# Latent attention with scores keys-on-partitions in split passes, query maxima as an operand row, row sums from ones beside the values

## The reference, cut to what matters

```python
def mla_queries(cq, g_q, w_uq, w_qr, rope):
    cq = rms_norm(cq, g_q)
    q_nope = (cq @ w_uq).reshape(b, n, MLA_HEADS, MLA_NOPE_DIM)      # 8 heads x 64
    q_rope = (cq @ w_qr).reshape(b, n, MLA_HEADS, MLA_ROPE_DIM)      # 8 heads x 32
    ...                                                              # rotated for latent tokens
def softmax_attend(q, k, v, scale):
    s = jnp.einsum('bqhd,bkhd->bhqk', q, k, preferred_element_type=jnp.float32) * scale
    p = jax.nn.softmax(s, axis=-1).astype(v.dtype)
    return jnp.einsum('bhqk,bkhd->bqhd', p, v)
```

## Time and profile before

| what | us |
|---|---|
| three runs, median (lowest, highest) | 3573.81 (3564.94, 3577.81) |
| the profiled execution, its own time | 3574.6 |
| its span, first to last instruction | 3572.5 |
| busy over the span: PE / PEld / DVE / ACT / POOL | 3058.5 / 2406.8 / 1741.1 / 1198.9 / 506.9 |
| granted TensorE clock, mean of the span | 0.918 of full |
| latent attention, first layer: setup, prologue, main part | 14.3, 9.6, 145.8 |
| latent attention, second layer | 15.7, 7.9, 124.0 |

### The profile page before, as it was taken

One profiled execution on the slowest core, in us unless ns is written; L12 is line 12 of the kernel. 1 busy time (PEld: TensorE's weight loads), 2 busy tenths in 40 slices (PEclk: granted clock), 3 DMA queues, 4 the chain that ended last, 5 costly groups with the idle time before them and its releaser, 6 DMA issues. The chain is left out here.

```text
span 3572.5 us, 39669 instructions
## 1 busy us (share of the span) xinstructions
PE 3058.5 (86%) x15861; PEld 2406.8 (67%) x15861; DVE 1741.1 (49%) x2631; ACT 1198.9 (34%) x1820; POOL 506.9 (14%) x425
## 2 busy tenths in 40 slices
PE   5679869799986999999699687997999968876995
PEld 3468545588875888888486545775788746554774
DVE  3664355423235554553610653335655443644886
ACT  4222344411113221221331544222322233533884
POOL 3240122200001000000230222001000013212331
PEclk9689989999997999999799999998999988885997
DMA  5774010122211443332261011332555414414961
GB/s 159 156 149 125 8 22 1 36 62 60 56 47 30 124 124 101 112 118 65 36 95 49 1 22 45 89 88 63 154 176 167 136 35 70 156 49 145 336 256 71
DMA packets 398239, 338.71 MB, mean 95 GB/s; under 512 B 38042, under 2 KB 338120, under 8 KB 397928
## 3 DMA queue, kind: packets, MB, share of 16 engines
q1 hardware_dynamic: 383272, 307.15, 29.8%
q0 software_dynamic: 14784, 29.03, 4.0%
HBM read 334.45 MB, written 36.22 MB: 104 GB/s over the span
## 5 line engine op out<-in xcount | busy, mean ns | idle before, releaser
L998 PE MATMUL ps<-ahi,w_hi 128*128 128x512 f32 (+1 forms) x2384 | 867.8, 364 | 165.5 <-DVE alo L666 84.4
L999 PE MATMUL ps<-ahi,w_lo 128*128 128x512 f32 (+1 forms) x2384 | 856.3, 359 | 0.0
L1000 PE MATMUL ps<-alo,w_hi 128*128 128x512 f32 (+1 forms) x2384 | 855.5, 359 | 0.0
L998 PEld LDWEIGHTS ps<-ahi,w_hi 128*128 128x128 f32 x2384 | 460.3, 193 | 253.0 <-issue 60.0
L1020 DVE TENSOR_TENSOR w_lo<-w_raw,w_hi 128x1024 fp32r<-128x1024 f32 (+2 forms) x248 | 359.1, 1450 | 437.0 <-ACT w_hi L1010 436.2
L1000 PEld LDWEIGHTS ps<-alo,w_hi 128*128 128x128 f32 x2384 | 460.0, 193 | 67.9
L999 PEld LDWEIGHTS ps<-ahi,w_lo 128*128 128x128 f32 x2384 | 461.2, 193 | 63.6
L1010 ACT CAST w_hi<-w_raw 128x1024 fp32r<-128x1024 f32 (+2 forms) x248 | 289.5, 1169 | 472.6 <-PE ps L1000 348.2
L832 DVE SCALAR_TENSOR_TENSOR vec_acc<-vec_w,csilu,vec_acc 128x512 f32<-128x512 f32 x364 | 262.9, 768 | 18.8 <-DMA vec_w<-in_w_mod 14.4
L1464 POOL TENSOR_SCALAR prob<-prob,nm 128x512 f32<-128x512 f32 (+4 forms) x104 | 164.4, 1580 | 674.4 <-DVE nm L1389 674.4
L1096 POOL TENSOR_TENSOR xsum<-x 128x768 f32<-128x768 f32 (+1 forms) x4 | 7.2, 1803 | 1482.3 <-DVE x L1081 1482.3
(11 more groups left out here) (433 smaller groups left out, 4948.2 us busy)
## 6 DMA issues: line engine op xcount, KB each, us to landing
vec_w<-in_w_mod SPq DMA_DIRECT2D x128, 512.0 KB, 4.1
w_raw<-in_w_in SPq DMA_DIRECT2D x104, 512.0 KB, 4.2
e_raw<-in_w_gate SPq DMA_DIRECT2D x46, 512.0 KB
e_raw<-in_w_up SPq DMA_DIRECT2D x46, 512.0 KB
e_raw<-in_w_down SPq DMA_DIRECT2D x46, 512.0 KB
w_raw<-in_w_ffn_gate SPq DMA_DIRECT2D x44, 512.0 KB, 3.8
w_raw<-in_w_ffn_up SPq DMA_DIRECT2D x44, 512.0 KB, 3.8
w_raw<-in_w_ffn_down SPq DMA_DIRECT2D x32, 704.0 KB, 4.7
```

The costliest lines, as they stand in the source:

```text
L998: pe.matmul(o, whi[:, j, b0 + b, :], hi[:, b, t0:t0 + tn], start=(b == 0), stop=False)
L999: pe.matmul(o, wlo[:, j, b0 + b, :], hi[:, b, t0:t0 + tn], start=False, stop=False)
L1000: m = pe.matmul(o, whi[:, j, b0 + b, :], lo[:, b, t0:t0 + tn], start=False, stop=(b == nb - 1))
```

## The change

`LatentHeads` takes the place of `Latent` and of `Heads` in the latent attention. It works on key tiles ("steps"): twelve for each pair of heads (six for each head), fourteen with context queries. Scores are computed transposed: a tile of 128 keys is the weights, all 512 queries move, and the result has keys on partitions, so that the exponential can go to the values without transposes. q and k are kept split (`qhi`, `qlo`, `khi`, `klo`, in fp32r) and multiplied in three passes. The row maxima come from **rough scores** (high x high alone, queries on partitions), one tile of 128 queries a step, ahead of their unit. VectorE's maxima stand in column 96 of `st`, a matmul with the identity turns them into a row (`row`), and ScalarE writes that, negated, as operand row 96 of `qhi`, against a row of ones in `khi`. The values' weights have 64 columns of values beside 64 of ones, so the sums come out in the other half of the partitions; ScalarE evicts both, VectorE takes reciprocals in parts of 256 columns, and GpSimd multiplies. A unit is now one head's 512 latent queries (j = 0, 1) or a pair's context queries (j = 2).

```diff
-        class Latent:
...
+        class LatentHeads:
+            COLS = 97
+            def __init__(self, c, proj, with_ctx, tensors):
...
+                span = 14 if with_ctx else 12
+                for i in range(4):
+                    for j, (kt, start) in enumerate(((6, 0), (6, 6), (2, 12))[:3 if with_ctx else 2]):
...
+                        if j < 2:
+                            first = -5 if u == 0 else i * span if j else (i - 1) * span + (8 if with_ctx else 6)
+                            places = [(first + t, t) for t in range(4)]
+                        else:
+                            places = [(i * span + 6 + t, t) for t in range(2)]
...
+                late = 2 if with_ctx else 0
+                plan = [(-8, "q", 0, 0), (-7, "kl", 0, 0), (-6, "kc", 0, 0), (-5, "q", 0, 1)]
+                for i in range(4):
+                    s = i * span
+                    if with_ctx:
+                        plan.append((s, "qc", i, 0))
+                    if i < 3:
+                        plan += [(s + late, "q", i + 1, 0), (s + late + 2, "kl", i + 1, 0), (s + late + 4, "kc", i + 1, 0), (s + late + 6, "q", i + 1, 1)]
...
+                def transposed_scores(s):
...
+                    if s >= 2:
+                        pe.wait_ge(*self.at(pt_done, s - 1))
...
+                        pe.matmul(ps[:, o:o + n], khi[0:self.COLS], qhi[0:self.COLS], start=True, stop=False)
+                        pe.matmul(ps[:, o:o + n], klo[0:MLA_K], qhi[0:MLA_K], start=False, stop=False)
+                        m = pe.matmul(ps[:, o:o + n], khi[0:MLA_K], qlo[0:MLA_K], start=False, stop=True)
+                def rough_scores(n):
...
+                    if n >= 1:
+                        pe.wait_ge(*self.at(nm_done[0], n))
...
+                            m = pe.matmul(ps[:, t0:t0 + tn], q, self.khi[0:MLA_K, i % 2, j, t0:t0 + tn], start=True, stop=True)
+                def project_piece(n):
...
+                    if n >= 5:
+                        pe.wait_ge(*self.at(prep_dve, self.dve_pos[n - 1, "low"]))
...
+                def values(s):
...
+                    pe.wait_ge(*self.at(pt_done, s + 1))
+                        m = pe.matmul(ps[:, bank:bank + LAT], weight(b, j), self.pt[:, s % 3, :], start=(b == 0), stop=(b == kt - 1))
...
+                for s in range(self.first, self.end):
+                    transposed_scores(s); rough_scores; row; project_piece; values(s - 1)      (each where its step has one)
...
+                # ScalarE, each step: exps(s), negated, rotated and high of the pieces, evict
+                # VectorE, each step: maximum, rotated_low, low, rotate of the pieces, one inverse of the queue
...
         def latent_attention(proj, l, with_ctx):
+                    @block.gpsimd
+                    def _(pool):
+                        pool.memset(vt[:, :, :, 1, :], 1.0)
+                        pool.tensor_copy(st[:], zero[:].unsqueeze(2).to_broadcast([P, 4, LatentHeads.COLS]))
+                        for s in range(2):
+                            pool.tensor_copy(khi[96:97, s], one.to_broadcast([1, 2 * ALL]))
...
-                            act.copy(vt[:, t, :], ps[:, BANK * (2 + t):BANK * (3 + t)])
+                            for h in range(2):
+                                act.copy(vt[:, t, :, 2 * h, :], ps[:, BANK * (2 + t):BANK * (3 + t)].rearrange("p (i h c) -> p i h c", i=4, h=2)[:, :, h, :])
+                            if t == 2:
+                                act.wait_ge(prep_dve.sem, prep_dve.base + 1)
+                                act.copy(khi[R0:R1].rearrange("p s h t -> p (s h) t"), k32[R0:R1].unsqueeze(1).to_broadcast([ROPE, 4, ALL]))
...
-                        for n in range(4):
-                            dve.tensor_tensor(k[R0:R1, n // 2, n % 2, 0:LAT], ra[R0:R1, :], rb[R0:R1, :], ALU.add)
-                            m = dve.tensor_copy(k[R0:R1, n // 2, n % 2, LAT:ALL], ps[R0:R1, LAT:ALL])
+                        dve.tensor_tensor(klo[R0:R1].rearrange("p s h t -> p (s h) t"), k32[R0:R1].unsqueeze(1).to_broadcast([ROPE, 4, ALL]),
+                                          khi[R0:R1].rearrange("p s h t -> p (s h) t").bitcast(F32), ALU.subtract)
...
-                attend(heads)
+                attend(LatentHeads(c, proj, with_ctx, (qhi, qlo, chi, clo, khi, klo, q32, ra, rb, rope, wq, wk, st, eye)))
```

More of the change, by code:

```diff
@@ L1590, in number_groups @@
                 n += u.last
-        class Latent:
[L1596 to L1669, removed]
-            def ended(self):
-                prep_mm.base += len(self.list)
-                prep_act.base += self.total["act"]
-                prep_dve.base += self.total["dve"]
@@ L1724, in _ @@
                     def _(act):
+                        act.copy(eye[:], ident[:])
                         for t in range(6):
                             act.wait_ge(pe_chain.sem, pe_chain.base + 2 + t)
-                            act.copy(vt[:, t, :], ps[:, BANK * (2 + t):BANK * (3 + t)])
+                            for h in range(2):
+                                act.copy(vt[:, t, :, 2 * h, :], ps[:, BANK * (2 + t):BANK * (3 + t)].rearrange("p (i h c) -> p i h c", i=4, h=2)[:, :, h, :])
+                            if t == 2:
+                                act.wait_ge(prep_dve.sem, prep_dve.base + 1)
+                                act.copy(khi[R0:R1].rearrange("p s h t -> p (s h) t"), k32[R0:R1].unsqueeze(1).to_broadcast([ROPE, 4, ALL])).then_inc(act_chain.sem, 1)
                     @block.vector
@@ L1746, in latent_attention @@
                 ld[3].base += 9 * 16
-                def mm_q(j, tok, n):
-                    def f(pe, i, bank):
-                        for kk in range(2):
-                            m = pe.matmul(ps[:, bank:bank + n], wq[:, kk, 2 * i + j, :], proj[:, T_CQ + kk, tok:tok + n], start=(kk == 0), stop=(kk == 1))
-                        return m
-                    return f
-                def mm_k(tok, n):
-                    return lambda pe, i, bank: pe.matmul(ps[:, bank:bank + n], wk[:, 2 * i * HD:2 * (i + 1) * HD],
-                                                         proj[:, T_CKV, tok:tok + n], start=True, stop=True)
@@ L1767, in out_q_plain @@
-                def out_q_plain(j):
-                    return lambda dve, ch, i, bank: dve.tensor_scalar(q[0:MLA_K, i % 2, j, LAT:ALL], ps[0:MLA_K, bank:bank + CTX], MLA_SCALE, None, ALU.mult)
-                def out_k(tok, n):
-                    def f(act, ch, i, bank):
-                        act.copy(k[0:HD, i % 2, 0, tok:tok + n], ps[0:HD, bank:bank + n])
-                        return act.copy(k[0:HD, i % 2, 1, tok:tok + n], ps[HD:2 * HD, bank:bank + n])
-                    return f
@@ L1793, in latent_attention @@
-                number_groups(units)
-                heads = Heads(c, units, per_bank=3, deep=False, out_banks=1, pieces=prep, negated=False, lag=1, dve_scales=(0,),
-                              before={"pe": prep.first_pe, "dve": lambda dve, ch: prep.first_out("dve", dve, ch),
-                                      "act": lambda act: prep.first_out("act", act, None)})
-                attend(heads)
-                prep.ended()
+                attend(LatentHeads(c, proj, with_ctx, (qhi, qlo, chi, clo, khi, klo, q32, ra, rb, rope, wq, wk, st, eye)))
```

320 lines of the change are left out of this document (287 added, 33 removed).

## The result

The changed kernel takes 3586.16 us (median of 8 runs, 3581.96 to 3589.97) against 3570.26 (8 runs, 3561.10 to 3577.81) in the same session: ratio 1.0046, 95% interval 1.0029 to 1.0064. The profiled execution took 3589.44 us, with a span of 3586.9.

A forecast was written before the change was run, and what follows sets the result against it. TensorE was near its limit, with matmul time about unchanged, so only waits could be gained. Setup, prologue, clock, main part and end summed to +6.8 (first layer) and +9.7 (second) on 3574.6: 3591 us, +0.46%, range 3568 to 3620.

The forecast's parts named there:

- Setup, +4.1: Setup of each layer: ScalarE's key-row spreading, then VectorE's low of 3,072 columns, end at 537.1 instead of 533.1 us.
- chain of 16.65 us: Prologue, first projection through rough scores, maxima, row and negation: 16.65 us, +7.1 in the first layer, +8.7 in the second.
- 3.1 us; I take 1.5: Prologue's clock term: nothing, or first q projection and four rough scores at 1.2 GHz, 3.1 us; 1.5 taken per layer.
- Main part, first layer: First score to last value matmul: 125.1 us of matmuls plus waits, switches and clock, 135.5 against 145.0, -9.5.
- Main part, second layer: First score to last value matmul: 101.5 us of matmuls plus waits, switches and clock, 113.4 against 123.0, -9.6.
- walk of four crowded steps: Second layer's main part: VectorE's 11.9 us against TensorE's 10.5 in four steps; TensorE loses 7 us over the pairs.
- The halved clock at the first unit ... again: Start of each main part: the halved clock costs 2.2 us before the change and was taken to cost that again.
- End, +3.6 and +5.0: After the last values: copies, reciprocals and a GpSimd product, 4.4 us against 0.8 (first layer), 5.8 against 0.69 (second).
- Exposed weight loads: Rival, main parts: each matmul group behind a wait pays 0.10 us, adding 11 + 13 us, total 3615; chance 0.26.
- Hidden prologue and no stalls: Rival: VectorE's 12 us backlog and all switches vanish and the clock holds, total 3570 us; chance 0.17.
- Faster: Rival: a gain over 18 us, needing wide f32 value matmuls below 0.86 us; at 0.6, 3565 or less; chance 0.08.
- Table loads: Rival, ScalarE: exponentials alternating with scaled Identity copies load tables at 1.28 us each, total about 3660; chance 0.03.

The follow-up runs named there:

- experiment 6: The changed kernel with rotated key rows spread after the first value tile, not the third, and the prologue's second q projection three steps later: 3578.30 us, 1.0022.
- experiment 2: The changed kernel plus matmuls that nothing reads, five ending each setup block and four, two, one in prologue gaps: 3582.31 us, 1.0033 of the kernel before.
- experiments 7 and 8: The changed kernel with the edits of experiment 4, experiment 5 and experiment 6 together, without and with useless matmuls: 3543.66 us (0.9931) and 3540.93 us (0.9905).
- experiment 8: The edits of experiment 4, experiment 5 and experiment 6 together, plus useless matmuls, three per setup and six in the prologue: 3540.93 us, 0.9905.
- experiment 5: The changed kernel with VectorE taking reciprocals only in steps without a row maximum, same work: 3580.90 us, 1.0027 of the kernel before.
- experiment 4: The changed kernel with probabilities and values rounded to fp32r, value matmuls in one pass instead of f32: 3562.30 us, 0.9970 of the kernel before.
- experiment 3: The changed kernel with each transposed score tile as one f32 matmul on rounded high parts instead of three fp32r passes: 3609.48 us, 1.0105.

## Why the prediction came out right

**The claim that carried it holds.** The main parts have about as many matmul microseconds as before (-2.9 in the first layer, +1.6 in the second), what they gained is waits (9.5 and 9.3 us), and setup, prologue and end, which had no cover, cost more than that. 1.0046 was measured where +0.46% was forecast. That two numbers agree so closely is luck: the terms missed by up to 2.9 us each and cancelled in part (the layers by -1.0 and +3.3), the stages sum to +18.8, not +16.5, and the unchanged code around them was 4.4 us faster in the traced execution. The 25 and 22 us of waits that the prediction had the kernel before lose were counted by columns; by busy time, which takes in switches and the matmuls' tails, they were 12.2 and 14.7, so the gain took most of what there was.

**Setup, +4.1:** +3.8 and +4.0. GpSimd's fills, costed at nothing, were done 13 us before the setup's end, as forecast; experiment 6 shows that ScalarE's copy behind the third value tile was the chain.

**Prologue, mis-sized by 2.1 and 1.7.** The chain of 16.65 us was about right for a full clock. In experiment 2, which has the same order and whose clock was up until the third maximum, the first rough score starts at 6.9 where I had 6.7, and without the wait behind useless matmuls the whole comes to an estimated 17. The term that was mis-sized is the clock's, "3.1 us; I take 1.5": by that estimate it was 3.2 and 2.8 here. In experiments 7 and 8, in another order, it was 3.3 and 4.0, and experiment 6 against experiment 8 gives 2.8 and 2.9. So it was about my upper bound, which had also left out k's projections, the maxima rows and the second q projection. By the Trainium skill (TensorE: Matmul & The Clock Gate, "What's actually happening"), activity has to release the throttled state. The trace agrees in the price and not in my reading "half clock throughout": the mean was 0.67, and the prologue paid nearly the full price because both q projections fell into the slow stretches, wholly or in part.

**Main part, first layer, -12.4 for -9.5.** Without waits I had 130.5 us; TensorE was busy 129.7. It waited 2.8, where I had counted 5.

**Main part, second layer, -7.6 for -9.6.** The walk of four crowded steps was right in kind: the waits end with VectorE, at a maximum and the lows behind it. They are 1.2 us in the first pair, 2.0 each in the second and third and 0.2 in the last, where I had 0.8, 2.6, 2.6 and 1; in the second and third pair it is the maxima row that waits for the maximum, not a rough score. All of TensorE's idle time there was 5.4, against 7. What was missing is that a wait can bring the clock down: 109.7 busy against my 106.4, and 106.6 in experiment 5, which has the same matmuls (its own first 12 us are at 0.75, a slower start than the change's 0.85). "The halved clock at the first unit ... again" was right at the first unit (0.73 and 0.85 in its first 12 us, first and second layer; 0.72 and 0.86 before) and not the whole.

**End, +3.6 and +5.0:** +3.7 and +4.7.

**The rivals.** *Exposed weight loads* fall: the plain step is 1.57 to 1.58, not 1.75, and experiment 4's matmuls follow one another by 0.23 to 0.24. *Hidden prologue and no stalls* falls on its first half (20 us, not under 12); its second half was nearly true in the first layer. *Faster* needed value matmuls below 0.86; they are not, and experiment 4 shows what it would have taken. *Table loads* fall: one load in each attention, though Identity copies alternate with exponentials. By the Trainium skill (ScalarE: Activation LUTs, "Table sets: the hidden batching unit") identity is in every table set. The trace agrees.

**What stays open.** Why the clock fell after one stall and not after another like it (experiment 2; in experiment 3 the two stalls are shorter, waits of 0.57 and 0.99, and neither was followed by a fall). Whether moving the second q projection pays at a full clock: 15.7 in experiment 8 against the estimate of 17 suggests some 1.3 us, and no run isolates it. The ends, 4.6 and 5.9 us, could be shortened by taking the last reciprocals in smaller parts, or the product on VectorE; neither was tried. Nor was a form that keeps the values' accuracy in split passes.

## What to carry to other kernels

Count a matmul's columns for every group of weights, idle halves included: fp32r passes were cheaper than f32 in the scores, and one wide f32 product with a ones block took it all back. A pipeline's fill and drain have no cover, so a change that deepens the chain of engines pays there in full, once for each stage, and here it paid part of it at the lower clock. Look at the clock in short windows: a mean over the stage hides which matmuls were slow. Put serial VectorE work (reciprocals, 1.75 us) into steps in which nothing waits for VectorE; here one condition on the order was worth 6 us of the second layer's 115; the kernel's median can't tell it apart.

## What the runs showed of the hardware that was not expected

- Two waits of about 1 us each within some 3 us of a dense stretch were followed by a granted clock of 0.86 over 12 us (the change, twice; experiment 6, 0.91 and 0.86), and the same matmuls took 3.2 us more over that main part than in experiment 5. In experiment 2 one such stall left the clock at 1.00.
- Over a whole prologue in which TensorE was busy 12.8 of 20.2 us the clock averaged 0.67: 0.50 in the first 6 us, after 4.55 us of idleness, then 0.93 over 4 us in which TensorE was busy for 1.65, then 0.50, 1.00 and 0.55. After 1.71 us of idleness (experiment 6) the first projection ran at the full clock, 1.96 us instead of 3.75. With 15.2 of 18.9 busy the mean was 0.91 (experiment 2), and 1.00 with 13.0 of 15.7 busy after matmuls that filled the wait ahead of it (experiment 8).
- The exponential of 512 columns takes 0.60 us without bias and row sum, where the one with both took 0.69. In a step of 1.57 it is hidden in both forms.
